# Three attention stages: the token tiles in another order, and four heads in one step for the two shortest

## The reference, cut to what matters

```python
# first block, each of two layers: 4 heads, two score maps per head
def block(args):                       # one tile of 128 queries
    s = jnp.einsum('bqhmd,bkhmd->bhmqk', qi, k)
    s = jnp.where(mask, s, -jnp.inf)   # keys up to the query's chunk of 64
    p = jax.nn.softmax(s, axis=-1)
    attn = p[:, :, 0] - lam * p[:, :, 1]
    return jnp.einsum('bhqk,bkhe->bqhe', attn, v)
# then rms_norm per head, times silu(z)

# second block: 8 heads, causal
def block(i):
    sc = jnp.einsum("bqhd,bkhd->bhqk", qn, k_nope) + jnp.einsum("bqhd,bkd->bhqk", qr, k_rope)
    p = jax.nn.softmax(jnp.where(causal, sc * scale, -jnp.inf), axis=-1)
    return jnp.einsum("bhqk,bkhd->bqhd", p, v)
```

## Time and profile before

| what | value |
| --- | --- |
| median of 3 runs | 2707.91 us (2706.21 to 2708.57) |
| the profiled execution: its own time, its span | 2705.85 us, 2704.1 us |
| PE / DVE / ACT / POOL busy, share of the span | 91% / 46% / 36% / 23% |
| first differential attention, from its first score to the next stage's first product | 514.32 to 643.84 us |
| second differential attention, its first score | 1152.71 us |
| MLA attention, from its first score to the next stage's first product | 1690.79 to 1859.83 us |
| mean granted clock of TensorE | 0.947 of full speed |

### The profile page before, as it was taken

How to read it: one execution, slowest core, us unless ns; L and a number is a source line. 1 busy time by engine, 2 the same in 40 slices (tenths; PEclk the granted TensorE clock), 3 DMA queues, 4 the chain that set the end, 5 groups by cost and what they waited for, 6 DMA issues and landing times. The chain is left out here.

```text
span 2704.1 us, 32904 instructions
## 1 busy us (share of the span) xinstructions
PE 2462.4 (91%) x13072; PEld 2012.8 (74%) x13072; DVE 1256.1 (46%) x1757; ACT 980.5 (36%) x2109; POOL 618.7 (23%) x281
## 2 busy tenths in 40 slices
PE   2799799788999799977999978998999999999998
PEld 2687587677878578766888877666878888888886
DVE  4794401585565400377444336662544434333336
ACT  3222422474532522366331255553632222122223
POOL 2210122032221112022232110111233333332331
PEclk9898799899999789979999988899999999999999
DMA  7342010002212111000321000002201211111113
GB/s 211 122 148 79 32 47 32 24 9 94 91 42 94 33 37 57 1 32 23 126 70 47 26 20 1 17 17 108 87 24 55 63 34 60 47 47 47 55 39 148
DMA packets 137998, 158.74 MB, mean 59 GB/s; under 512 B 7276, under 2 KB 104947, under 8 KB 137845
## 3 DMA queue, kind: packets, MB, share of 16 engines
q1 hardware_dynamic: 135437, 152.12, 17.2%
q10 hardware_dynamic: 2408, 4.52, 0.5%
HBM read 135.65 MB, written 20.97 MB: 58 GB/s over the span
## 5 line engine op out<-in xcount | busy, mean ns | idle before, releaser
L698 PE MATMUL ps<-hT_hi,w_hi 128*128 128x512 f32 x1184 | 464.5, 392 | 23.5 <-PEq L369 12.7
L698 PE MATMUL ps<-hT_lo,w_hi 128*128 128x512 f32 x1184 | 463.3, 391 | 0.0
L698 PE MATMUL ps<-hT_hi,w_lo 128*128 128x512 f32 x1184 | 463.0, 391 | 0.0
L698 PEld LDWEIGHTS ps<-hT_hi,w_hi 128*128 128x128 f32 x1184 | 223.6, 189 | 71.2 <-issue 24.8
L698 PEld LDWEIGHTS ps<-hT_hi,w_lo 128*128 128x128 f32 x1184 | 223.6, 189 | 46.5
L698 PEld LDWEIGHTS ps<-hT_lo,w_hi 128*128 128x128 f32 x1184 | 223.7, 189 | 46.2
L698 PE MATMUL ps<-w_hi,hT_hi 128*128 128x512 f32 (+1 forms) x640 | 244.2, 382 | 2.1 <-PEq L927 2.1
L698 PE MATMUL ps<-w_lo,hT_hi 128*128 128x512 f32 (+1 forms) x640 | 243.8, 381 | 0.0
L698 PE MATMUL ps<-w_hi,hT_lo 128*128 128x512 f32 (+1 forms) x640 | 243.4, 380 | 0.0
L634 POOL TENSOR_TENSOR w_lo<-ffn_raw,w_hi 128x2048 fp32r<-128x2048 f32 (+1 forms) x32 | 163.9, 5121 | 112.0 <-ACT w_hi L608 112.0
L3418 DVE TENSOR_SCALAR work<-work,fcols 128x1024 f32<-128x1024 f32 x44 | 33.3, 756 | 287.7 <-ACT work L3375 287.7
(11 more groups left out here) (485 smaller groups left out, 5016.8 us busy)
## 6 DMA issues: line engine op xcount, KB each, us to landing
ffn_raw<-in_ffn_w_up SPq DMA_DIRECT2D x40, 512.0 KB, 5.1
mix_gla<-in_w_ada SPq DMA_DIRECT2D x32, 512.0 KB, 3.8
difp_raw<-in_w_in SPq DMA_DIRECT2D x12, 1024.0 KB, 4.9
big<-xres SPq DMA_DIRECT2D x3, 4096.0 KB, 16.3
xres<-big SPq DMA_DIRECT2D x24, 512.0 KB, 2.6
ffn_raw<-in_ffn_w_down SPq DMA_DIRECT2D x10, 1024.0 KB, 5.0
ada_raw<-in_w_ada SPq DMA_DIRECT2D x16, 512.0 KB, 5.8
glap_raw<-in_w_in SPq DMA_DIRECT2D x8, 1024.0 KB, 5.1
```

The source lines that it names most:

```text
L698: mm = nc.tensor.matmul(out, l, r, start=(job.part != 1 and c == 0 and k == 0), stop=(job.evac and c == job.chunks - 1 and k == 2))
```

## The change

The tiles go in the order 0, 4, 5, 1, 6, 2, 7, 3. Tiles 0 and 1 take all four heads (or pairs) in one step, tiles 2 and 3 take two as before, tiles 4 to 7 one. There are 22 steps: tile 0 is s0, tile 4 is s1 to s4, tile 5 is s5 to s8, tile 1 is s9, tile 6 is s10 to s13, tile 2 is s14 and s15, tile 7 is s16 to s19, tile 3 is s20 and s21. What used to be counted by tile (the buffers of y, the passes after a tile is complete) now goes by *rank*, the tile's place in this order. `mix` and `z` are still addressed by the tile itself.

In the differential attention all low parts of held weights go to POOL, and the pieces have passes 4, 8, 9 and 14. The raw weights lie where tiles 2, 3, 6 and 7 will be written, so each load is now two DMAs of 256 columns. In the MLA a step of four pairs does its scores pair by pair, with the rotary part and the mask right behind each, and PE asks for the second half of the rotary queries at s1 instead of s8.

```diff
-    STEP = {2: (0, 1), 3: (2, 3), 12: (4, 5), 13: (6, 7)}
-    BY_VECTOR = (2, 3)
+    STEP = {4: (0, 1), 8: (2, 3), 9: (4, 5), 14: (6, 7)}
...
             if t:
                 sp.wait_ge(self.s_lo, self.PIECES * t)
-            sp.dma_start(self.raw[:, :, :], job.srcs[0]).then_inc(self.s_raw, 16)
+            for e in range(2):
+                sp.dma_start(self.raw[:, :, e, :], job.srcs[0][:, :, 256 * e:256 * e + 256]).then_inc(self.s_raw, 16)
...
         for n in self.STEP.get(step, ()):
-            act.wait_ge(self.s_raw, 16 * (n // self.PIECES + 1))
+            act.wait_ge(self.s_raw, 32 * (n // self.PIECES + 1))
...
-    def __init__(self, H):
-        self.all = attention_steps(H)
+    ORDER = (0, 4, 5, 1, 6, 2, 7, 3)
+
+    def __init__(self, four=(0, 1, 2, 3)):
+        sets = {4: [four], 2: [(0, 1), (2, 3)], 1: [(h,) for h in range(4)]}
+        self.all = [(r, heads) for r, i in enumerate(self.ORDER) for heads in sets[4 if i < 2 else 2 if i < 4 else 1]]
         self.n = len(self.all)
-        self.last = {i: max(n for n, (j, _) in enumerate(self.all) if j == i) for i in range(NT)}
+        self.last = {r: max(n for n, (q, _) in enumerate(self.all) if q == r) for r in range(NT)}
...
-                if n in held.BY_VECTOR:
-                    held.low(dve, n)
...
-                if n not in held.BY_VECTOR:
-                    held.low(pool, n)
+                held.low(pool, n)
...
-    st = Steps(MLA_H // 2)
+    st = Steps((0, 2, 1, 3))
...
-            if n == st.last[3] + 1:
+            if n == 1:
                 up.second_half(pe)
+            if len(st.heads(n)) < 4:
+                for part in parts(n):
+                    plain(n, part)
+                return
+            for k in (0, 2, 1, 3):
+                part = parts(n)[k]
+                plain(n, part)
+                rotated(n, [part])
+                mm = masked(n, k)
+            mm.then_inc(s_s, 1)
```

More of the change, by code:

```diff
@@ L1435, in rows, with half, blocks, ends @@
         return flat.rearrange("p (k s) -> p k s", k=nh)[:, :, 0:W]
[L1437 to L1444, removed]
+    def half(self, flat, n, part):
+        nh, W = len(self.heads(n)), self.width(n)
+        if nh == 4:
+            return flat.rearrange("p (k s) -> p k s", k=2)[:, :, 0:W]
+        return flat[:, 0:W] if nh == 2 else flat[:, 0:W - 512 if part else 512]
+    def blocks(self, n, part):
+        nh = len(self.heads(n))
+        every = [(k, j, S // nh * k + P * j) for k in range(nh) for j in range(self.tile(n) + 1)]
+        return [b for b in every if b[2] // 512 == part]
+    def ends(self, n):
+        return [r for r in range(NT) if self.last[r] == n]
 def stage_diff_attention(nc, m, v, z, mix, next_jobs):
     H = DIFF_H
-    st = Steps(H)
+    st = Steps()
     n_steps = st.n
@@ L1490, in y_of @@
             h0 = st.heads(n)[0]
-            return y[st.tile(n) % YB][:, P * h0:P * h0 + P * len(st.heads(n))]
+            return y[st.rank(n) % YB][:, P * h0:P * h0 + P * len(st.heads(n))]
         def ends(n, lag):
-            return [i for i in range(NT) if st.last[i] == n - lag]
-        def blocks(n, part):
-            return [b for b in st.blocks(n) if b[2] // 512 == part]
+            return st.ends(n - lag)
         @block.sync
@@ L1549, in values @@
                     pe.wait_ge(s_eb, n + 1)
-                for k, j, c in blocks(n, part):
+                for k, j, c in st.blocks(n, part):
                     h = st.heads(n)[k]
@@ L1606, in finish @@
             def finish(n):
-                i, nh = st.tile(n), len(st.heads(n))
+                i, nh = st.rank(n), len(st.heads(n))
                 dve.wait_ge(s_o, n + 1)
@@ L2808, in parts @@
         W = st.width(n)
-        if len(st.heads(n)) == 2:
+        if len(st.heads(n)) > 1:
             return [(k, pair, 0, W) for k, pair in enumerate(st.heads(n))]
         return [(0, st.heads(n)[0], k0, min(W, k0 + 512)) for k0 in range(0, W, 512)]
-    def blocks(n, part):
-        return [b for b in st.blocks(n) if b[2] // 512 == part]
-    def transposed(n, part):
-        return 512 * part, st.bank_cols(n)[part]
-    def ends(n):
-        return [i for i in range(NT) if st.last[i] == n]
     def toks(i):
@@ L2932, in empty @@
         def empty(n, mp, part):
-            c, w = transposed(n, part)
             if part == 0:
@@ L2954, in _ @@
                 empty(n - 1, 1, 0)
-            for i in ends(n - 2):
+            for i in st.ends(n - 2):
                 empty_y(i)
```

81 lines of the change are left out of this document (47 added, 34 removed).

## The result

The changed kernel took 2716.26 us (median of 8 runs, 2710.22 to 2719.27) against 2706.98 us before: a ratio of 1.0031, 95% interval 1.0021 to 1.0042. I had predicted 2707.8, that is, no difference that can be told. The range of 2695 to 2717 holds the result, but the likeliest case is wrong: it is **slower by 9.3 us**. In a second series, further down, the same kernel came out at 1.0017 (1.0008 to 1.0026). Why the two series differ is taken up in the experiments and isn't settled in full.

A forecast was written before the change was run, and what follows sets the result against it. PE, busy 91% of the span, was taken as the bound. Two differential stages at +1.7 us each (+3.4) and the MLA at −3.5 gave −0.1 us: 2707.8 us against the median 2707.9, range 2695 to 2717.

The forecast's parts named there:

- bounds of −8 and +1: MLA stage: limits in us around the predicted −3.5; −8 stood for a clock that doesn't fall.
- rival D: Tile 4, three stages: low clock stays throughout, +3 us per stage, +8.9 in all, 2716.8 us; chance 0.1.
- The third term, 108.0: MLA, from the start of tile 5 until s21 is reached: predicted to take 108.0 us together.
- 4.0 + 2.4 = 6.4 us: Differential stage, second weight load: PE waits 4.0 us, then loses 2.4 us at half clock.
- 0.4 us in my sum: Differential stage: DVE slowed by two more pairs of low parts on POOL, 0.4 us, between 0 and 2.2.
- the 1.8 us that I set beside the page: Differential stage: by the skill's shared-SBUF page, both POOL pairs paid in full, sum 1.8 us higher per stage.
- The end: +3.7: Differential stage's end: 2.7 us chain for tile 7 plus 1.0 for s21, 3.7 us, bounds 2.0 to 4.5.
- 8.8: Differential stage, first score to last step's score: old path 105.36 us, new 96.6, a gain of 8.8 us.
- A: Differential stages: no wait for the second load, −4.7 us per stage, 2695 us; chance 0.15.
- B: Differential stages: the load wait comes but the clock doesn't fall, 4.8 us lower, 2703 us; chance 0.17.
- C: Differential stages: half loads land one after the other, +6.7 us per stage, +9.9 in all, 2717.8; chance 0.12.
- E: Whole kernel: PE and DVE work, not waits, set stage length; terms below 2 us, 2708; 0.46 with main case.

The follow-up runs named there:

- sums_first: old_mla with the sum of squares ahead of `finish` in each DVE pass of the differential stages: 2705.83 us, 0.9995 of the kernel before.
- both_old_mla: old_mla with the third pair of weight pieces in pass 11 instead of 9 and the sums ahead of `finish`: 2698.23 us, 0.9969 of before.
- old_mla: The changed kernel with its MLA stage put back to the 24 rising steps: 2707.81 us, 1.0004 of the kernel before.
- only_mla: The kernel before with the new order and steps in the MLA only: 2708.57 us, 1.0012 of the kernel before.
- mla_fill2: The changed kernel with five and four cheap unread products ahead of the MLA's waits of s1 and s2: 2704.27 us, 0.9992 of before.
- best_fill: The changed kernel with later weight pieces, sums ahead of `finish`, and fillers at s1 and s2 of MLA and differential stages: 2688.64 us, 0.9936 of before.

## Why the prediction was wrong

**The MLA, where it failed.** The step was "s0 with four pairs and its chain 5.5 (bounds as above), s1 7.4 at half clock with 1.9 us of wait, s2 6.9, s3 6.2, s4 6.5: tile 5 begins 32.5 us after the stage's start", with bounds of −8 and +1. Tile 5 began after 43.9 us in the first profile and 37.0 in the second. By terms, first and second profile:

| | predicted | first | second |
| --- | --- | --- | --- |
| s0 | 5.5 | 8.7 | 8.7 |
| s1, s2 | 7.4, 6.9 | 6.5, 8.4 | 6.5, 8.4 |
| s3, s4 | 6.2, 6.5 | 10.7, 9.6 | 7.6, 5.9 |
| s5 to s21 | 108.0 | 111.4 | 111.3 |

Two things were wrong in it. First, s0: I took the size of the differential stage's step for it. But four pairs have four scores of the plain and the rotary kind, and these alone took 6.4 us, in the middle of which the clock fell. That is 3.2 us. Second, the clock: I let it come back with s3, as "dense work brought it back within 6 us" in the differential stage. In the MLA it came back in s3 in one execution and at the end of s4 in the other, there with PE busy for 32.43 of 35.18 us. Two waits of 2.32 and 1.83 us near the start are where it can be helped: filled, the clock is back in s1. The lower bound of −8 (no fall of the clock) was fair, but the upper one of +1 left out what I had given a chance of 0.1 as rival D. **Rival D is what happened, in the MLA alone**, over all of tile 4 in the first profile and up to s3 in the second. My price for it, 3 us for each of three stages beyond my terms, was spread over the wrong places: nothing in the differential stages, and in the MLA tile 4 took 35.2 or 28.35 us where my terms have 27.0, so 8.2 or 1.4 us. The third term, 108.0, was 3.4 us low. 1.1 of it is tile 1's step of four pairs (9.7 for 8.6), 1.0 is tile 6 (28.1 for 27.1), 0.7 is tile 2 and 0.5 tile 5; what makes tile 6 longer wasn't tried.

**The differential stages.** Predicted +1.7 each, measured +0.4. The path to s21 was right to about a microsecond: 102.4 us against 96.6 + 0.4 + 4.0 + 2.4 = 103.4. Part of that is luck, since tile 6 came out 2.5 us shorter than its terms and tiles 2 and 7 2.1 us longer. The two losses were the ones named, and each was then removed by itself. The second load: I had 4.0 + 2.4 = 6.4 us, and its removal gave 3.8. ACT waited for 3.94 us, not 4.5, PE for 2.66, not 4.0, and the half clock behind it lasted 3 us of products, not 5. The rule of the Trainium skill that I had set beside it (TensorE: Matmul & The Clock Gate, HAM oscillation: matmuls behind a wait for a DMA start cold) agrees with these rows, at the smaller size; the wait on PE was ended by ACT, which had waited for the load.

What the low parts on POOL cost DVE, 0.4 us in my sum, no run isolates. But I had read the earlier trace rows wrongly. The combine of 2.13 us at 587.89 didn't stand beside the low parts. POOL had finished them and was at its product with z:

```profile
584.35 2.50 POOL L1403 TENSOR_TENSOR w_lo<-mix_diff,w_hi 128x512 fp32r<-128x512 f32 x2 [1.16 <-ACT w_hi L1397]
...
587.92 1.29 POOL L1651 TENSOR_TENSOR att_y<-att_y,zd 128x512 f32<-128x512 f32 x1
```

In the changed kernel a combine at 568.25 had low parts beside it for 0.4 us and took 1.15 us, as it did with POOL idle. So neither my bounds nor the 1.8 us that I set beside the page follow from these rows. What the low parts did lengthen is the small product ahead of the combine: at 582.46, in the kernel before, it took 0.75 us instead of 0.22.

The end: +3.7 predicted, +3.4 measured, and its 2.7 us chain went with sums_first (27.60 to 24.89 us). The gain of the rest was put too high: 8.8 less 0.4 and less the 1.0 of the end is 7.4; both_old_mla shows 5.7 us. Tile 4 came out at 16.5 (17.1), tile 1 at 5.4 (5.15), tile 2 at 10.5 (9.2), tile 7 at 19.0 (18.2).

**The other rivals.** A (no wait) and B (no fall of the clock) fall by the rows of the second load. C (the halves one after the other) falls too: the second load was complete 5.0 us after its first issue, where C needed 8.3. E (nothing moves) was right by accident for each differential stage: 5.7 us gained, some 6 lost.

**The sum.** Per differential stage +0.4, the MLA +4.0 or +10.9, so +5 or +12 us in all, plus what the clock does in untouched code (+2.5 us in the first profile). The two series have medians of +9.3 and +2.9, which fits two different mixtures of early and late returns. What stays open: how the shares of early and late returns come about, since old_mla (+1.8) and only_mla (+2.6) together are less than the +9.3 of the first series; and whether the new order would match the old one in the MLA if its clock never fell. In mla_fill2 and best_fill it still fell in s0, and 168.0 against 164.8 us holds that fall too. The four series of experiments ran on chips 11, 0, 15 and 0, each beside the kernel before; whether the shares depend on the chip wasn't tried. And a profile shows one execution: the MLA stage of the old order (169.0 and 171.4 us) and the untouched code between the differential stages (508 to 511 us) differ by 2 to 3 us between profiles.

## What to carry to other kernels

Ask which work a reordering puts into the stretch where the clock is low, and price both candidates there at both levels: the short tiles lost 5.7 us to it and the long one 6 to 13. At a stage's start, a wait of 2 us on TensorE that is filled with work nobody needs can be worth more than a new order; take the cheap form of product and no more of it than the wait holds. And when a sum moves two losses into the same place as the gain, remove them one at a time before the change is given up: the rest of the change paid 5.7 us per differential stage once both were gone.

## What the runs showed of the hardware

- The same instructions took 173.0 and 179.9 us in one stage of one kernel, by when the clock of 2.4 GHz came back (in s3 or at the end of s4). The times of that kernel lie in two groups, some 6 us apart, which fits it but isn't shown run by run.
- A stretch in which PE is busy for 32.43 of 35.18 us can stay at 1.2 GHz. Busy time alone didn't tell when the clock returns; in the differential stage it was back in tile 4 after waits of the same length.
- The clock fell 2.4 us after the start of the MLA stage in both profiles of the changed kernel, and ten fp32 transposes as fillers brought it back at the same place, in s1, as five products did.
- Five fillers of identity times fp32 data took 6.05 us where the clock came back among them and 4.51 us at the full clock; five of the operands that the kernel rounds to its high parts took 2.48 us at the half clock.
- A load of 1 MB as two DMAs of 512 KB on one queue, issued 0.4 us apart, was complete 5.0 us after its first issue; the same load as one DMA took 4.8 us.
- A DVE instruction of 1.02 us (the combine of 768 keys) took 2.13 us beside POOL's product with z; one of 1.15 us (896 keys) took 1.15 us beside POOL's low parts.
